# Two transformer blocks on one core: dense products between the blocks of the transition products in the recurrent stage

## What is computed

```python
def step(s, inp):
    r_t, w_t, k_t, v_t, kk_t, a_t = inp
    sa = jnp.einsum('bhij,bhj->bhi', s, -kk_t)
    s = (s * w_t[:, :, None, :] + sa[..., None] * (kk_t * a_t)[:, :, None, :]
         + v_t[..., None] * k_t[:, :, None, :])
    return s, jnp.einsum('bhij,bhj->bhi', s, r_t)
```

## Time and profile before

| | |
|---|---|
| median of 3 runs | 3571.59 us (3570.25 to 3573.34) |
| the profiled execution | 3570.03 us, its span 3567.9 us |
| PE busy | 3429.4 us, 96% of the span, 25549 MATMULs and 25549 weight loads |
| DVE busy | 2336.5 us, 65% |
| ACT busy | 564.0 us, 16% |
| mean granted clock of the PE | 0.985 |

### The profile page before, as it was taken

The page is one execution under the profiler, slowest core; times in us unless marked ns, Lnnn a source line. Parts: engine busy times, 40 slices in busy tenths (PEclk is TensorE's granted clock), DMA queues, the critical chain, the costliest instruction groups (busy, mean ns, idle before and its releaser), DMA issues. The chain is left out here.

```text
span 3567.9 us, 59508 instructions
## 1 busy us (share of the span) xinstructions
PE 3429.4 (96%) x25549; PEld 2763.8 (77%) x25549; DVE 2336.5 (65%) x4471; ACT 564.0 (16%) x1072; POOL 162.6 (5%) x168
## 2 busy tenths in 40 slices
PE   7998989899999999999999999999999999999999
PEld 4455656577788888889998866767877888888888
DVE  2277778776559889999777645555753656644644
ACT  2232222222001000000002132222221000000000
POOL 1000000000000000000001010000001000000000
PEclk9999999999999999999999999999999999999999
DMA  9833333344587878786665644544324776654543
GB/s 336 259 84 103 91 96 106 106 118 123 185 280 234 264 251 259 238 258 201 213 206 184 212 142 142 166 142 143 117 71 138 228 235 194 224 174 164 177 165 130
DMA packets 662389, 638.53 MB, mean 179 GB/s; under 512 B 42466, under 2 KB 629728, under 8 KB 661104
## 3 DMA queue, kind: packets, MB, share of 16 engines
q1 hardware_dynamic: 553440, 563.15, 49.2%
q10 hardware_dynamic: 108016, 71.44, 6.9%
q0 software_dynamic: 672, 0.15, 0.0%
HBM read 628.41 MB, written 6.29 MB: 178 GB/s over the span
## 5 line engine op out<-in xcount | busy, mean ns | idle before, releaser
L2007 PE MATMUL bank<-work,extra 128*128 128x256 f32 x2112 | 463.0, 379 | 0.0
L664 DVE SCALAR_TENSOR_TENSOR work<-weight_ring,silu_c,work 128x256 f32<-128x256 f32 x1050 | 450.5, 501 | 0.0
L2007 PEld LDWEIGHTS bank<-work,extra 128*128 128x128 f32 x2112 | 400.9, 190 | 53.9
L2007 PE MATMUL bank<-weight_ring,work 128*128 128x256 f32 x1408 | 316.3, 383 | 8.1 <-ACT work L2140 7.5
L2208 DVE TENSOR_TENSOR work<-weight_ring 128x2048 f32<-128x2048 f32 (+2 forms) x72 | 129.7, 1801 | 294.0 <-DMA weight_ring<-in_w_gate_up 155.6
L2007 PEld LDWEIGHTS bank<-weight_ring,work 128*128 128x128 f32 x1408 | 268.2, 192 | 45.3 <-issue 8.3
L1012 PE MATMUL bank<-work,x_channels 128*128 128x256 f32 (+1 forms) x704 | 245.2, 489 | 0.0
L2754 PE MATMUL bank<-work,weight_ring 128*128 128x512 f32 x448 | 203.9, 600 | 1.1 <-PEq L2450 1.1
L1012 PEld LDWEIGHTS bank<-work,x_channels 128*128 128x128 f32 x704 | 130.4, 195 | 76.0 <-issue 63.5
L2007 PE MATMUL bank<-weight_ring,extra 128*128 128x256 f32 x704 | 159.3, 379 | 4.0 <-DVE extra L2203 4.0
L2007 PE MATMUL bank<-work 128*128 128x256 f32 x704 | 159.2, 379 | 0.0
(11 more groups left out here) (463 smaller groups left out, 5498.9 us busy)
## 6 DMA issues: line engine op xcount, KB each, us to landing
weight_ring<-in_w_mod SPq DMA_DIRECT2D x80, 2048.0 KB, 10.1
weight_ring<-in_w_gate_up SPq DMA_DIRECT2D x44, 2048.0 KB, 9.4
weight_ring<-in_w_in SPq DMA_DIRECT2D x26, 2048.0 KB, 9.9
weight_ring<-in_w_gate SPq DMA_DIRECT2D x22, 2048.0 KB, 8.4
weight_ring<-in_w_up SPq DMA_DIRECT2D x22, 2048.0 KB, 13.3
weight_ring<-in_w_down SPq DMA_DIRECT2D x20, 2048.0 KB, 8.1
weight_ring<-in_w_mod ACTq DMA_DIRECT2D x32, 1024.0 KB, 6.3
weight_ring<-in_w_out SPq DMA_DIRECT2D x16, 2048.0 KB, 10.4
```

Of the source, the lines that this page charges most:

```text
L664: ins = v_.scalar_tensor_tensor(a, w[:, k, :], c, a, ALU.mult, ALU.add)
L2007: last = mm(product(u, p), right[p][:, k, :], left[p][:, k, :], start=k == 0, stop=k == 7)
```

## The change

The table gets a new entry `within`, 0.9 us, and `transitions` calls `fill` with it in front of each of its blocks but the first, so three times in a call and six times in a pass. The entries for the place between the two calls and for the place in front of the read rows get smaller (4.4 to 2.6 and 3.0 to 0.4).

```diff
-FILL = {"first solve": 8.0, "first": 3.0, "value": 7.0, "ahead": 6.0, "solve": 7.0, "centre": 2.0, "round": 2.2, "gram": 2.5, "between": 4.4, "rows": 3.0, "chain": 1.5, "step": 0.55}
+FILL = {"first solve": 8.0, "first": 3.0, "value": 7.0, "ahead": 6.0, "solve": 7.0, "centre": 2.0, "round": 2.2, "gram": 2.5, "within": 0.9, "between": 2.6, "rows": 0.4, "chain": 1.5, "step": 0.55}
...
                 for x in range(4):
+                    if x:
+                        fill(FILL["within"])
                     tile, d = 2 * tp + x // 2, x % 2
```

## The result

The changed kernel takes 3578.15 us (median of 20 runs, 3569.22 to 3594.59), the kernel before in the same comparison 3570.86 (20 runs, 3562.86 to 3576.06). The ratio is 1.0025 with a 95% interval of 1.0017 to 1.0033: slower by about 9 us, 7 by the medians. The prediction said 3570 with "same" as likeliest. "Slower" had a chance of 0.24 there. The profiled execution of after took 3582.87 us, 12.8 more than that of before, and its span is 3580.3, 12.4 more; it stands 4.7 us above the median of its kernel, so the traces show more of a difference than the medians do.

A forecast was written before the change was run, and what follows sets the result against it. The PE, busy 96% of the span, bounds the kernel, with page waits and low clock. Windows -2.3, earlier dense work -6.0, chain step 6 -4.6 and clock +11 gave -1.9 us: 3570, 8-in-10 range 3555 to 3587.

The forecast's parts named there:

- same: Whole kernel: the summed terms hold, -1.9 us, a time of about 3570; chance 0.46 as a case, 0.49 as an outcome.
- Slower: Whole kernel: outcome of a time above that of the kernel before by more than 0.2%, 7 us; chance 0.24.
- the clock: Idle stretches at read rows and page waits: half of thirteen bring the low clock at 1.8 us each, 11 us.
- read rows pull the clock down: Read rows: the new 2.3 us wait brings 1.2 GHz every pass, 26 us instead of 11, 3585; chance 0.17.
- The windows: First transition product to read rows, all eight passes: 154.6 us at full clock, 2.3 less than 156.9.
- The small parts: Inside the windows: block alone 0.73 us, each split 0.35, read-row wait 2.3 in passes 1 to 7.
- The chain: Behind the read rows: dense work done earlier saves 6.0 us, the vanished wait at chain step 6 another 4.6.
- The page: First calls: the PE's next 256 instructions arrive behind the weight transfer, 6.9 us after the start in pass 1; waits total 12.4.

The follow-up runs named there:

- busy_rows: The changed kernel with five dense products that nobody reads put into the idle stretch in front of the read rows; 3561.80 us.
- front_heavy: first_only with most dense products of the first place moved inside the first call (`within` 1.75, `between` 1.2, `step` 0.4); 3549.26 us.
- rows_only: The kernel before with only the entry `rows` cut from 3.0 to 0.4, no block split; 3593.13 us.
- rows_back: The changed kernel with the entry `rows` put back to 3.0, blocks still split; 3568.86 us.
- half_small: The kernel before with one of the two 1 MB transfers in front of the transitions cut to an eighth; 3565.69 us.
- late_loads: The kernel before with both 1 MB transfers in front of the transitions held back until the first call has ended; 3574.74 us.
- steps_only: The kernel before with 0.4 us instead of 0.55 of dense work per chain step and nothing else; 3598.81 us.
- even: The changed kernel with `rows` back at 3.0, all splits kept, and `step` 0.2 instead of 0.55; 3554.68 us.
- first_only: The changed kernel with `rows` at 3.0, dense products between the blocks of the first call only, and `step` 0.45; 3556.42 us.
- even_first: first_only with 0.35 instead of 0.45 us of dense work per chain step; 3570.15 us.

## Why the prediction was wrong

It named the mechanism and mis-sized one term. It forecast 1.9 us less than before, with "same" as likeliest, and the kernel is slower.

- **The step that failed** is the clock: "The new idle stretches (2.3, and 1.9 to 3.5) are near the 1.94 and 1.95 that went either way, so I take half, 11 us." The low level came behind the read rows in six of the seven passes with a wait of 2.20 us, and behind four page waits, ten stretches where half of thirteen had been counted. Those at the read rows cost 2.3 us each on average where 1.8 had been taken. Together that is 13.6 + 8 = about 22 us, 11 more than the term. Filling the idle stretch at the read rows (busy_rows) gives 11.4 us back in the chains. This is the recorded rival *read rows pull the clock down*, with its own point of decision, ten of thirteen stretches or about 20 us. Its full price of 26 us was too much, and so was its 3585 against the median of 3578. Two idle stretches that went one way each were too few for a half.
- **The windows.** Forecast 154.6 without the clock, measured 168.0 - 8 = 160. Of the 5.4 missing, pass 0 holds 1.8: its page wait of 1.51 us was left out of its sum, though the trace of before has it too (1.53 us), as was the chance of new waits. The page waits of passes 1 to 7 are 3.21, 1.45 and 1.23, 3.20, 1.92, 1.26 and 2.31, together 14.6 against 12.4 forecast. Pass 6's 1.26 and the second wait of pass 2 had been taken as none. The single values stood at 2.7, 1.9, 3.5, 2.4 and 1.9, so the reasoning about what lies ahead of a boundary held, and front_heavy shows it again by an edit.
- **The small parts** were right: block 0.73 forecast, 0.76 measured; two dense products 0.86 + 0.20, measured 1.07; read-row wait 2.3, measured 2.20 (2.83 in pass 0 against 2.9); pass 3 17.5, measured 17.93. So a split costs about what was said where it stands. That it is a loss on balance is not so: rows_only, without splits, is 15 us slower than after, and before and rows_back can't be told apart.
- **The chain.** The 6.0 and 4.6 us did come: the wait of 1.12 us in step 6 is gone in all four passes, pass 3 went from 20.76 to 18.59 us, and in busy_rows the chains sum to 147.6, 10.6 below before. That this is the forecast to the tenth is partly luck: pass 0 gave 1.4 us that were not forecast, and pass 7 gave none. In after the low clock takes the gain back.
- **The page.** That the page comes "as a fixed delay behind that transfer" is shown, by half_small, late_loads, front_heavy and the landings of the packets, for passes 1, 2, 4 and 5. In pass 7 the transfer in the way is another one, the 2 MB that SyncE issues. The delay has a part that no transfer explains: about 4 us after the start of the call with 0.08 MB in flight. The Trainium skill, "Runtime: NRT & Kernel Launch", section "Instruction fetch mechanics", calls the cost of crossing a block boundary mostly hidden. For most boundaries the traces agree: of the 202 pages of before ten in the recurrent stage begin with a wait over 0.7 us. For the first calls they don't: late_loads has 1.85 to 2.12 us there with hardly a transfer beside the page, and before has 4.86 with 2 MB.

## What to carry to other kernels

Price an idle stretch of the PE with the clock that may follow it. Here 2.2 us idle cost 1.6 to 3.0 us more in six passes of seven, and two stretches of 2.1 and 2.2 us in steps_only some 7 us more each, by the growth of their chains less that of the waits. Products that fill such a stretch can be free even if nobody reads them (busy_rows). Before moving work, list for each place the wait that the work covers (copies, a page of instructions, a late transfer), and leave as much there as the wait is long. Here six products fewer at the read rows cost 22 us by themselves. With them back, and what the chain steps give spread so that some is left for its end, even and first_only gained some 20 us over the kernel before. It isn't a safe gain: steps_only, which has such a spread and nothing within the first call, is 27 us slower than before, and even_first, which differs from first_only by 0.1 us in one entry, is no faster than before.

## What the runs showed of the hardware that was not expected

- An idle stretch of 2.20 us brought the 1.2 GHz level in six of seven passes and not in pass 3, with the same instructions around it. In rows_only the same wait at the same place (2.21 us in passes 1 and 5) brought no fall. What tells them apart stays open.
- The low level can last 20.4 us though the PE is busy in 19.97 of them (steps_only); 9.4 us of that is dense products, the rest small ones and the first products of the next pass. Behind the read rows of after, with four dense products following, it lasted 3.4 to 6.8.
- The level can also fall with no long idle stretch: in the chain of pass 1 of rows_back small products stood at most 0.51 us apart, and the clock was at 1.2 GHz from 384.3 to 394.6 us.
- A page's wait ends 1.2 to 1.6 us after its packet has landed, in all 127 such waits over 0.7 us in the recurrent stage of the thirteen traces.
- With hardly a transfer beside it the page boundary in the first call still costs about 2 us, the page arriving 3.8 to 4.4 us after the start of the call. Holding back the transfers removed part of that wait, and waits grew at the next boundary, to 5.23 us in the worst case (pass 3 of late_loads).
